# Delta-rule phase of a hybrid decoder step: where two projection pieces, the residual and the turn of the last output stand in a tile

## What is computed

```python
kk = jnp.einsum('nbhik,nbhjk->nbhij', k_beta, kc) * seg
a_mat = jnp.eye(L, dtype=F32) + jnp.where(strict, kk, 0.0)
sol = lax.linalg.triangular_solve(a_mat, rhs, left_side=True, lower=True)
u, w = sol[..., :V], sol[..., V:]
...
v_new = u_c - jnp.einsum('bhik,bhkv->bhiv', w_c, S)
o = jnp.einsum('bhik,bhkv->bhiv', q_d, S) + jnp.einsum('bhij,bhjv->bhiv', a_c, v_new)
S = S * jnp.exp(bl)[..., None] + jnp.einsum('bhjk,bhjv->bhkv', k_o, v_new)
...
o = rms_norm(o, g_norm).reshape(B, T, -1)
y = (o * jax.nn.silu(z.astype(F32))).astype(h.dtype) @ w_out
x = (x.astype(F32) + gate * rms_norm(y, g_post[l])).astype(x.dtype)
```

## Time and profile before

| | us |
|---|---|
| median of 3 runs | 3077.59 (3073.18 to 3078.0) |
| the profiled execution | 3075.56 |
| its span | 3073.7 |
| PE busy in the span | 2721.0 (89%) |
| DVE, ACT, POOL busy | 1386.6, 962.9, 765.3 |
| the delta-rule phase's 16 tiles | from about 2248 to 2959 of the span |

### The profile page before, as it was taken

The page is one execution under the profiler, slowest core; times in us unless marked ns, Lnnn a source line. Parts: engine busy times, 40 slices in busy tenths (PEclk is TensorE's granted clock), DMA queues, the critical chain, the costliest instruction groups (busy, mean ns, idle before and its releaser), DMA issues. The chain is left out here.

```text
span 3073.7 us, 55105 instructions
## 1 busy us (share of the span) xinstructions
PE 2721.0 (89%) x21280; PEld 1610.5 (52%) x21280; DVE 1386.6 (45%) x3076; ACT 962.9 (31%) x2795; POOL 765.3 (25%) x840
## 2 busy tenths in 40 slices
PE   8588999999689998539899999997599999999997
PEld 1133444444456666224344444445478778788783
DVE  0232121120156773438535263544366566665635
ACT  0243323221211110034313122212455555555531
POOL 0134010100211110025400000000465564555621
PEclk9789999999789997569999999999699999999976
DMA  7434021101433331035411111111543132232212
GB/s 265 164 103 144 28 91 46 65 28 70 130 117 127 130 118 48 28 91 164 137 43 66 49 62 59 49 55 30 160 119 92 58 96 71 78 98 62 72 36 69
DMA packets 263834, 270.20 MB, mean 88 GB/s; under 512 B 31694, under 2 KB 199006, under 8 KB 263583
## 3 DMA queue, kind: packets, MB, share of 16 engines
q1 hardware_dynamic: 191756, 231.98, 23.1%
q10 hardware_dynamic: 71872, 35.28, 4.6%
HBM read 179.89 MB, written 87.33 MB: 87 GB/s over the span
## 5 line engine op out<-in xcount | busy, mean ns | idle before, releaser
L475 PE MATMUL inc_b<-inc_h,inc_w_hi 128*128 128x512 bf16 (+3 forms) x1920 | 485.2, 347 | 32.8 <-issue 11.3
L475 PE MATMUL inab_b<-inab_w_hi,inab_h 128*128 128x512 f16 (+1 forms) x1088 | 330.4, 384 | 13.0 <-POOL inab_w_lo L455 13.0
L475 PE MATMUL inc_b<-inc_h,inc_w_lo 128*128 128x512 bf16 (+1 forms) x960 | 315.0, 347 | 0.0
L475 PEld LDWEIGHTS inc_b<-inc_h,inc_w_hi 128*128 128x128 f16 x1920 | 170.0, 99 | 218.9 <-issue 29.4
L475 PE MATMUL inab_b<-inab_w_lo,inab_h 128*128 128x512 f16 (+1 forms) x544 | 208.9, 384 | 0.0
L475 PE MATMUL inab_b<-inab_h,inab_w_hi 128*128 128x512 bf16 (+3 forms) x720 | 183.0, 349 | 16.9 <-DVE inab_h L421 16.9
L475 PE MATMUL inc_b<-inc_w_hi,inc_h 128*128 128x512 f16 (+3 forms) x816 | 176.4, 314 | 15.0 <-POOL inc_w_lo L455 14.3
L475 PEld LDWEIGHTS inab_b<-inab_w_hi,inab_h 128*128 128x128 bf16 (+1 forms) x1088 | 108.4, 100 | 144.6 <-issue 20.9
L1632 DVE SCALAR_TENSOR_TENSOR inc_acc<-inc_ub,inc_taps,inc_acc 128x512 f32<-128x512 f32 (+1 forms) x240 | 167.5, 698 | 8.6
L1547 ACT ACTIVATE inc_ub<-inc_b 128x512 f32<-128x512 f32 x96 | 57.3, 597 | 320.6 <-PE inc_b L475 320.6
L475 PEld LDWEIGHTS inc_b<-inc_h,inc_w_lo 128*128 128x128 f16 x960 | 93.9, 99 | 93.4 <-issue 4.9
(11 more groups left out here) (384 smaller groups left out, 5927.9 us busy)
## 6 DMA issues: line engine op xcount, KB each, us to landing
ada_w<-in_w_ada SPq DMA_DIRECT2D x12, 2048.0 KB, 8.4
tmp_qkv<-inc_so SPq DMA_DIRECT2D x96, 256.0 KB, 2.0
mixc_qkv<-tmp_qkv SPq DMA_DIRECT2D x15, 1536.0 KB, 7.6
inc_stage<-in_w_in_c ACTq DMA_DIRECT2D x32, 512.0 KB
inab_stage<-in_w_in_ab ACTq DMA_DIRECT2D x24, 512.0 KB, 4.0
inab_x<-in_x_prompt SPq DMA_DIRECT2D x16, 512.0 KB, 3.2
tmp_v<-inab_vz SPq DMA_DIRECT2D x32, 256.0 KB, 3.5
tmp_z<-inab_vz SPq DMA_DIRECT2D x32, 256.0 KB, 2.0
```

What stands on the lines that cost most here:

```text
L475: last = nc.tensor.matmul(dst, lhs(a, k), rhs(b, k), start=(k == 0 and i == 0), stop=(k == KT - 1 and i == len(PASSES) - 1))
```

## The change

Four things are moved, nothing is added or taken away.

1. Pieces 4 and 5 of the second half of a projection leave the end of PE's body and go between the widths of the next tile: pieces 4 to 7 now stand beside k = 0 to 3, the last two between a Y product of group 0 and the T and N products of group 1. In the short tile two pieces each stand at its two places.
2. The square goes from behind k = 0 to behind k = 4 on ACT, and the two halves of the decays from k = 3 and 4 to k = 2 and 3.
3. The two halves of the product with the gate go on DVE from k = 3 and 4 to behind the widths, ahead of `gate`. The root and the residual on POOL keep their place in its order.
4. `turn_o` goes on PE from ahead of `across_n` to behind `state_keys`; on ACT `first_outputs` goes ahead of `oT_copy`.

```diff
@@ ACT
             def beside(k):
-                if k == 0 and early >= 2:
+                if k in (2, 3):
+                    decays(t + 1, nxt, n2, k - 2)
+                if k == 4 and early >= 2:
                     fin.square(act, t - 2, P, 1)
-                if k >= 3:
-                    decays(t + 1, nxt, n2, k - 3)
...
+            first_outputs(t, P, par)
             if early >= 1:
                 oT_copy(t - 1, P)
-            first_outputs(t, P, par)
@@ DVE
-            levels(t, BOTH, LEVELS, (lambda k: gated(t - 2, P, k - 3) if k in (3, 4) else None) if early >= 2 else (lambda k: None))
+            levels(t, BOTH, LEVELS)
+            if early >= 2:
+                gated(t - 2, P, 0)
+                gated(t - 2, P, 1)
@@ PE, levels
             for k in range(1, len(widths)):
                 y_product(t, k, 0, halves, widths)
+                if 2 <= k < 4:
+                    beside(k)
                 tn_products(t, k - 1, 1, halves, widths)
                 tn_products(t, k, 0, halves, widths)
                 y_product(t, k, 1, halves, widths)
-            beside(2)
+            beside(4)
@@ PE, body
             def beside(k):
-                if k < 2 and t >= 2:
-                    fin.project(pe, t - 2, P, 1, [6 + k])
-                if k == 2:
+                if k < 4 and t >= 2:
+                    fin.project(pe, t - 2, P, 1, [4 + k])
+                if k == 4:
                     turn_k(t + 1, nxt, half, n2, 0)
...
             state_outputs(t, par)
+            across_n(t)
+            state_keys(t, par)
             if t >= 1:
                 turn_o(t - 1, P)
-            across_n(t)
-            state_keys(t, par)
...
             query_keys(t + 1, nxt, n2)
-            if t >= 1:
-                fin.project(pe, t - 1, P, 1, range(4, 6))
@@ PE, the short tile
-        levels(nt, LOW, LEVELS[:2], lambda k: fin.project(pe, nt - 2, P, 1, [6 + k]) if k < 2 else None)
+        levels(nt, LOW, LEVELS[:2], lambda k: fin.project(pe, nt - 2, P, 1, range(4 + 2 * k, 6 + 2 * k)) if k < 2 else None)
```

## The result

The changed kernel takes **3084.38 us** (median of 22 runs, 3069.43 to 3090.36) against 3077.52 for the kernel before (22 runs, 3069.56 to 3083.93): a ratio of 1.0021, 95% interval 1.0012 to 1.003. It is slower, by some 6.5 us (the medians differ by 6.9), where 3071.0 was forecast; the median lies outside the range, and the interval holds no ratio under 1. The profiled execution has a span of 3082.2 us, against 3073.7.

What follows compares the result with a forecast made beforehand. PE was taken to bound the tile outside the widths, and a chain of PE, DVE and ACT widths 2 to 4. 0.83 - 1.30 = -0.47 us a tile, 14 times -6.6, from 3077.59 gave 3071.0 us; range 3065.5 to 3080.5.

Steps and rivals of the forecast that it cites:

- Removed at the tile's end: End of PE's tile: taking pieces 4 and 5 away saves 1.30 us a tile, with no wait exposed behind them.
- Added in the widths: Widths k = 2 and 3: the pieces push the chain by 0.38 and 0.45, together 0.83 us a tile.
- Square, root, gate: ACT and DVE behind the widths: the later square and gate, taking 2.17 or 3.15 us, stay hidden, barely by the second.
- The turn of the last output: PE's last group: the turn, some 1.0 us, goes behind the state's key products at no cost.
- POOL behind the residual: POOL after the residual of 4.23 us: key products wait 0.3, scaled values stay hidden with 0.3 us left.
- a gate near 2.2 with a residual near 4.2: Sign expected in the trace: DVE's gate takes about 2.2 us and POOL's residual about 4.2.
- rival C: DVE loses one more turn to POOL, so PE's state products wait 1.1 us; +0.63 a tile, 3086.4 us, chance 0.12.
- B: Rival: the chain in the widths takes the pieces in full, 1.50 added; +0.2 a tile, 3080.4 us, chance 0.11.
- D: Rival: more gain, a switch before the Y product goes and widths expose 0.55; -0.84 a tile, 3065.8 us, chance 0.12.
- The sum: Whole kernel: 14 tiles at -0.47 us each make -6.6 us, giving 3071.0 us from the median of three runs.

Runs made afterwards that it cites:

- e1: The changed kernel with POOL's residual moved behind the next key's scales and weighted decays; 3070.73 us, ratio 0.9981 to the kernel before.
- e2: The changed kernel with the gate on DVE put ahead of the two halves of the product with the gate; 3073.32 us, ratio 0.999 to the kernel before.
- e7: e1 with the turn of the last output back ahead of the upper-right product on PE; 3074.77 us, ratio 0.9988 to the kernel before.
- e3: The changed kernel with only the turn of the last output back ahead of the upper-right product on PE; 3105.45 us, ratio 1.0093 to the kernel before.
- e8: e1 with projection pieces 4 and 5 left out of every prompt tile; 3055.09 us, ratio 0.9926 to the kernel before.
- e6: The kernel before with only POOL's residual moved behind the weighted decays; 3076.02 us, ratio 0.9989 to the kernel before.

## Why the prediction was wrong

- **Removed at the tile's end**, 1.30: right, 1.29. Nothing was exposed behind it.
- **Added in the widths**, 0.83: right in kind, 0.91 in size (1.34 and 1.35 from Y product to products instead of 1.31, so 0.41 and 0.49 for the widths instead of 0.38 and 0.45). With this alone the period would be 47.04, as e1 and e2 show, and the time some 5.5 us under that of before.
- **Square, root, gate** is the step that failed. The start was right (DVE began the gate 22.48 us after the tile's first Y product; 2697.6 - 2675.08 = 22.52 was forecast), and so was the time at which DVE is wanted for the copy (25.6 forecast, 25.8 in e1). The duration was not: 2.17 was taken from the last tile, with 3.15 of the steady tile as the other end, and the step's "hidden, barely by the second value" was tested against these two only. It was 4.33. Both bounds came from places where the two instructions met in another order: in the last tile the residual waited, and before the change it began ahead of the gate and held only its first operation (1.31 us; the earlier trace rows). The prediction took the gate as one holder that comes first and keeps the residual out; it is eight operations, and the residual got in behind the first. The upper end stood in the same rows: the gate alone and the residual alone, 2.17 + 2.36 = 4.53. With that, DVE is free at 2697.6 + 4.53 = 2702.1 where it was wanted at 2700.7, and the step would have read a stall of up to 1.4.
- **The turn of the last output**, cost nil: the forecast held in e7's setting. With the long gate it was a gain of over 1 us a tile (e3), which kept the loss small; no step of the prediction has this.
- **POOL behind the residual.** Half of this step rests on a residual of 4.23, which was 2.36: of "a gate near 2.2 with a residual near 4.2", both were the other way. The weighted decays started at 2711.38, 28.1 after the tile's first Y product instead of 27.2, but DVE's key products, late themselves, didn't wait for them. So rival C was right in kind, a turn of DVE lost to POOL, and wrong in its place: its sum has late scaled values, but PE's state products had no idle entry; the copy of the upper-right product was late, the other entry that the prediction's signs name for C. That its 3086.4 came near the measured time is luck, since it prices another wait. B fell: a width with a piece takes 4.17, under the 4.3 that B asks for, and e8 gives 0.45 a piece, not B's 0.75. D fell too: the widths took 0.91, not 0.55, and the end gave 1.29, not 1.39.
- **The sum**: the terms 1.30 and 0.83 measured 1.29 and 0.91; the missing term is +0.83 a tile, 14 x 0.83 = 11.6 us. The forecast of -6.6 us turned into about +6 (-6.6 + 11.6, and 14 x 0.09 = 1.3 for the two terms).

## What to carry to other kernels

When a DVE operation with two SBUF inputs and a POOL operation that reads SBUF are moved beside each other, price the overlap as the sum of both and put it on each engine in turn; a duration read where they met in another order is no bound. Then look what stands right behind on each engine: a hold of 0.95 us was free where DVE had 3.66 to spare even with it (before, e6), and one of 4.33 - 2.18 = 2.15 cost 0.83 a tile where DVE had 1.19 to spare without it (e1). A POOL instruction that nobody waits for belongs where the other engine has no such operation, and a run of short DVE operations need not keep it out.

## What the runs showed of the hardware

- In all 14 steady tiles a POOL instruction that started 0.16 to 0.25 us into a run of eight back-to-back DVE operations got in at the next seam and held DVE for its whole length (2.49 us for one operation of 0.34). Two POOL instructions in a row took turns with DVE's operations (1.41 and 1.36).
- At one place, the short last tile, POOL waited in all twelve kernels through all of the gate's operations instead (4.23; 3.15 for a half; 2.08 for 8 columns). None of the runs explains it.
- The effects of two moves don't add: the turn's place is worth 1.1 us a tile beside the long gate (49.0 in e3 against 47.86, at the full clock) and some 0.1 beside the short one (e7), the residual's place 0.82 behind the change and nothing in the tile before it (e6).
- In e3, with a wait of PE of 1.15 and one of 0.35 us in each tile, the granted clock fell to 0.50 behind them in some tiles, which then lasted 3.1 us longer; in the changed kernel, with one wait of 0.56 a tile, it stayed at 1.00 through the phase.
